# Moving one buffer by 128 bytes: split weights that begin 192 bytes past a multiple of 512 in place of 64

## The reference

```
# block 1, two layers: attention, then a pooling mixer, each followed by an MLP
x = x + moba_attention(rms_norm(x, g), w_qkv, w_o, cos, sin)
x = x + squared_relu_mlp(rms_norm(x, g), w_up, w_down)     # 1024 -> 4096 -> 1024
x = x + pool_mixer(rms_norm(x, g), w_groups, scale)
x = x + squared_relu_mlp(rms_norm(x, g), w_up, w_down)
x = rms_norm(x, g)
# block 2: a state-space branch and a latent-attention branch on one input projection,
# gated and merged; then cross attention to a memory of 256 rows;
# then 32 experts, each 1024 -> 256 -> 1024, two for each token; then a last norm
act = silu(t @ w_gate[e]) * (t @ w_up[e]) * combine
```

## Time and profile before

| | |
|---|---|
| three runs | 1241.28, 1235.68, 1241.53 us; median 1241.28 |
| the profiled execution | 1234.28 us, of which the span is 1232.5 |
| mean granted clock of TensorE | 0.993 |
| TensorE busy | 1179.9 us (96%), 9056 matmuls |
| VectorE busy | 783.6 us (64%) |
| ScalarE busy | 608.3 us (49%) |
| DMA | 270.28 MB, mean 219 GB/s |

### The profile page before, as it was taken

How to read it: one execution, slowest core, us unless ns; L and a number is a source line. 1 busy time by engine, 2 the same in 40 slices (tenths; PEclk the granted TensorE clock), 3 DMA queues, 4 the chain that set the end, 5 groups by cost and what they waited for, 6 DMA issues and landing times. The chain is left out here.

```text
span 1232.5 us, 22410 instructions
## 1 busy us (share of the span) xinstructions
PE 1179.9 (96%) x9056; PEld 1000.1 (81%) x9056; DVE 783.6 (64%) x1316; ACT 608.3 (49%) x993; POOL 100.0 (8%) x102
## 2 busy tenths in 40 slices
PE   9999999999999999999999989999999999999992
PEld 7989999999999999899999988899999833333320
DVE  6876655566755566999899889879655552221213
ACT  6665554455544554767655576665554331111101
POOL 0000100000200000000000030010100004341301
PEclk9999999999999999999999999999999999999997
DMA  9654566564456656445444384365543999999993
GB/s 303 203 172 137 189 189 198 185 196 146 162 181 195 193 182 197 137 152 173 155 137 138 109 274 139 104 205 168 186 160 124 421 360 412 417 413 414 412 404 130
DMA packets 161045, 270.28 MB, mean 219 GB/s; under 512 B 17625, under 2 KB 126142, under 8 KB 156862
## 3 DMA queue, kind: packets, MB, share of 16 engines
q1 hardware_dynamic: 149872, 260.53, 60.6%
q0 software_dynamic: 10720, 8.42, 2.3%
q10 hardware_dynamic: 366, 0.12, 0.0%
HBM read 287.89 MB, written 13.63 MB: 245 GB/s over the span
## 5 line engine op out<-in xcount | busy, mean ns | idle before, releaser
L2128 DVE TENSOR_TENSOR weights_parts<-ring,weights_parts 128x1024 fp32r<-128x1024 f32 (+3 forms) x312 | 363.5, 1185 | 138.4 <-ACT weights_parts L1546 138.0
L1546 ACT ACTIVATE weights_parts<-ring 128x1024 fp32r<-128x1024 f32 (+3 forms) x312 | 309.1, 1011 | 144.6 <-PE psum L885 143.9
L883 PE MATMUL psum<-xnorm_parts,weights_parts 128*128 128x256 f32 x852 | 243.4, 286 | 6.8 <-DVE arena L2531 3.2
L884 PE MATMUL psum<-xnorm_parts,weights_parts 128*128 128x256 f32 x852 | 237.5, 279 | 0.0
L885 PE MATMUL psum<-xnorm_parts,weights_parts 128*128 128x256 f32 x852 | 237.5, 279 | 0.0
L883 PE MATMUL psum<-expert_cols,weights_parts 128*128 128x256 f32 (+1 forms) x688 | 192.5, 280 | 3.5 <-DVE expert_cols L2146 2.2
L884 PE MATMUL psum<-expert_cols,weights_parts 128*128 128x256 f32 (+1 forms) x688 | 190.1, 276 | 0.0
L885 PE MATMUL psum<-expert_cols,weights_parts 128*128 128x256 f32 (+1 forms) x688 | 190.1, 276 | 0.0
L883 PE MATMUL psum<-hidden_parts,weights_parts 128*128 128x256 f32 x640 | 178.7, 279 | 3.0 <-DVE hidden_parts L2599 1.7
L884 PE MATMUL psum<-hidden_parts,weights_parts 128*128 128x256 f32 x640 | 177.1, 277 | 0.0
L885 PE MATMUL psum<-hidden_parts,weights_parts 128*128 128x256 f32 x640 | 177.1, 277 | 0.0
(11 more groups left out here) (452 smaller groups left out, 1723.8 us busy)
## 6 DMA issues: line engine op xcount, KB each, us to landing
ring<-in_mlp_w_up SPq DMA_DIRECT2D x32, 1024.0 KB, 5.4
ring<-in_mlp_w_down SPq DMA_DIRECT2D x32, 1024.0 KB, 4.8
ring<-in_w_in SPq DMA_DIRECT2D x30, 1024.0 KB, 5.1
ring<-in_attn_w_qkv SPq DMA_DIRECT2D x12, 1024.0 KB, 6.0
expert_raw<-in_w_exp_gate SPq DMA_DIRECT2D x22, 512.0 KB
expert_raw<-in_w_exp_up SPq DMA_DIRECT2D x22, 512.0 KB
ring<-in_w_exp_down SPq DMA_DIRECT2D x9, 1024.0 KB
expert_raw<-in_w_exp_down SPq DMA_DIRECT2D x9, 1024.0 KB
```

Of the source, the lines that this page charges most:

```text
L883: pe.matmul(out, lh, rh, start=start, stop=False, **more)
L884: pe.matmul(out, lh, rl, start=False, stop=False, **more)
L1546: ins = act.activation(high, src, ACT.Copy)
L2128: ins = dve.tensor_tensor(low, src, high.bitcast(F32), ALU.subtract)
```

## The change

The call that makes `dskip_all` moves ahead of the two that make the weights buffer. With its 128 bytes in front, `weights_parts` and `expert_weights` begin at byte 193,728 of a partition (378 x 512 + 192) and no longer at 193,600 (378 x 512 + 64). `dskip_all` itself goes from byte 226,368 to 193,600. `ssd_par` and all behind it, and all ahead of `dskip_all`, keep their addresses. No instruction changes its place on any engine: 6034 rows of TensorE, 950 of VectorE, 731 of ScalarE, 71 of GpSimd and 271 of SyncE stand in the order in which they stood.

```
--- before.py
+++ after.py
@@ -394,10 +394,10 @@
         results = sb("results", [P, M_END - M_COLS])
         arena_rest = sb("arena_rest", [P, ARENA - M_END])
         half_rows = sb("half_rows", [P, 2, 2 * MORE], I32)
+        dskip_all = sb("dskip_all", [P, SH])
         with nc.sbuf_tensor("expert_weights", [P, 2 * UNITS * UNIT], F32) as w_plain:
             pass
         w_parts = sb("weights_parts", [P, 2 * UNITS * UNIT], F32R)
-        dskip_all = sb("dskip_all", [P, SH])
         ssd_par = sb("ssd_par", [SH, 4])
         std_col = sb("std_col", [P, 2, TB])
         gain_both = sb("gain_both", [P, KT])
```

## The result

The changed kernel has a median of 1247.84 us over 8 runs (1240.26 to 1252.12), the kernel before 1237.97 over 8 (1232.67 to 1242.39). The ratio is 1.0084, with a 95% interval from 1.0059 to 1.0108. I had forecast no change, with 1239 us and a chance of 0.14 for slower.

A forecast was written before the change was run, and what follows sets the result against it. TensorE was taken to set the pace ahead of the expert stage, DMA queues from 1000 us. Terms for TensorE, VectorE with ScalarE, and DMA summed to 0, keeping 1234.28 us; 1239 was forecast, between two groups of runs, range 1230 to 1250.

The forecast's parts named there:

- What bounds the kernel: TensorE sets the pace ahead of the expert stage, DMA queues from 1000 us; TensorE's changes ahead pass on nearly in full.
- VectorE, ScalarE, the expert stage's matmuls at 0: Splitting the weights and streaming them in the expert stage cost 0; VectorE and ScalarE within 0.5 us each way.
- DMA at 0: Expert loads into the weights buffer take no longer: 0, with ends of -2.7 and +2.7 us.
- the sign: In the expert stage, 412 GB/s from 1000 to 1100 us would show the forecast right.
- My estimate of 1.6 us of 244: Expert-stage writes into the weights buffer 1.6 us slower if the page's rule for reads held; not taken into the sum.
- TensorE, split products, at 0: The 6996 split matmuls keep their two paces, 113.3 and 117.7 ns: 0, with ends of +21 and -9.5 us.
- 64 against 0 as a bound for 192: Rows comparing starts 64 and 0 on TensorE, VectorE and ScalarE, differing by 0 to -10 ns, stood in for start 192.
- The slower rival: Fast split matmuls turn slow, above all the MLP's: 13.5 us, 1252 us; all 4800 quick ones 21 us, 1260; chance 0.18.
- The slow share of 2170: Of 6996 split matmuls, some 2170 have the slow pace, 281 ns duration, and would stay near that count.
- The marks: Signs of right or wrong, such as MLP's 1008 matmuls in 114.24 us (right) or 118.6 us (wrong, the slower rival).

The follow-up runs named there:

- the first small kernel: Split matmuls alone, computation left out, each stretch behind a wait, stationary and moving starts each 0 to 448 bytes in steps of 64; 113.3 to 120.0 ns per matmul.
- the version with two starts: Kernel before with a 128-byte gap between high and low weights, high parts at 64, low at 192: 1233.60 us, ratio 0.9929; again 1232.06 us, 0.9964.
- the one at 0: Kernel before with half_rows laid behind the weights, so the weights begin at 0 like the other large buffers: 1265.01 us, ratio 1.0201.
- the one at 320: Kernel before with a gap of 256 bytes ahead of the weights, which begin at 320, others at 0: 1239.85 us, ratio 1.0022.

## Why the prediction was wrong

- **What bounds the kernel**: right. TensorE's pace ahead of the expert stage is what the change touched, and between 0.7 and 0.9 of it reached the end.
- **VectorE, ScalarE, the expert stage's matmuls at 0**: right, 1241, 1054 and 592 ns. **DMA at 0**: right for this buffer. The first 100 us of the sign, 1000 to 1100, have 404 GB/s in place of 412, 394 up to 1050 us and 414 behind it, as the stage begins later. What the stage takes is the same: from the first to the last matmul from the weights buffer 187.5 and 187.7 us in two executions before, 187.6 and 187.8 in two after. My estimate of 1.6 us of 244, from the Trainium skill's page DMA: Bandwidth & Descriptors, section "How a descriptor splits into AXI transactions", would be 1.2 us of this span, and the traces don't bear it out.
- **TensorE, split products, at 0**: this step failed. It said "One start that has both paces says that something else picks between them", and went from there to a price of 0 with a weight of 0.62. Something else does pick between two paces, the moment of entry. But the start decides which paces there are to pick from, and how often each is picked: at class 64 both, at class 192 nearly always 117.8 from a wait or a short lead (0 of 96), at 0 and 128 the quick one never (0 of 191 stretches in the first small kernel). Two outcomes at one setting only show that the setting doesn't fix the outcome; they leave open that it sets the odds.
- **64 against 0 as a bound for 192**: the nearest rows were the wrong ones. All of them (592 ns, 1217 ns, 620 ns) are of work in which TensorE doesn't read two SBUF operands in this close order, or which isn't TensorE's at all. In the split products no row of before had stationary and moving operand at another distance than 64 or -64, and I did not say that this left 0 and 128, now known to be 5 to 7 ns worse than the quick pace, without any row. What I also missed: with the period of 256, -64 is 192, the distance to which the change takes the stationary weights. The products with the weights moving were rows of it. By their start times 398 of 469 ran slow before, against 1685 of 6402 with the weights stationary; the earlier trace rows show it as means of 278 and 279 ns. They are short stretches, and even at 64, after the change, 270 and 353 of them ran slow, so this alone would not have settled the price.
- **The slower rival** was the right mechanism: "the places that are fast now can turn slow, above all the MLP". Its price, 13.5 us for the MLP and 21 for everything, is that of the second execution of the changed kernel, where the matmuls took 19.7 us more (117.53 against 114.71 ns, x 6996) and the time was 17.9 us longer. In the first, the MLP's loops stayed quick and it was 8.9 and 6.0. The median lies between. I had given it 0.18 because no row said what picks a pace; that lack should have counted for it as much as against it.
- **The slow share of 2170**, worked out from means of durations, was 2091 by the start times. The same sum wouldn't do after: at 192 the slow pace has 279 ns, not 281.
- **The marks**: "1008 matmuls of the MLP in 118.6 us" didn't come in the first trace and did in the second; with one trace of the changed kernel, that mark would have spoken for the wrong case.
- **The time**: 1247.84 lies inside the range of 1230 to 1250, but the direction was missed.

## What to carry to other kernels

Where a kernel reloads the stationary operand for every matmul, look at the starts of the stationary and the moving operand modulo 256 bytes, and sweep them with a kernel of a few hundred bare matmuls: here the first such run ranked the starts 0, 128, 192 and 64 as the full kernel did, over a range of 2%, and a later one found the version with two starts, 0.4 to 0.7% under the kernel before. Count matmul starts in equal stretches, since means of durations hide two paces. And when one setting shows two outcomes, ask what sets their odds before giving the setting a price of nothing.

## What the runs showed that I had not expected

- The pace of back-to-back 128x128 by 256 split matmuls depended on (stationary start - moving start) mod 256: 120.0 ns at 0, 113.3 or 117.8 at 64, 118.2 to 119.1 at 128, 117.8 and sometimes 113.3 at 192. At 64 it was not the difference alone that picked.
- Of 16 starts in steps of 16 bytes, 113.3 ns came only at 64 and 192.
- Which of two paces a stretch takes is settled within its first few matmuls and then kept, for over 1000 of them in the MLP; it differs between executions of one program. I take this for the main part of the scatter of 10 us in the runs before (the version with two starts spreads over 4 us, the one at 0, which has one pace, over 2.5 us in six runs, and the one at 320, which has two, over 17 us in twelve), which the line through the executions supports and no run proves.
- With all large buffers at 128 in place of 0 the expert stage, which the DMA sets, took 4.4 and 4.7 us more (404 and 407 in place of 414 GB/s); with the weights buffer moved alone it took no more.
- What inside TensorE or SBUF makes the classes stays open; no run here shows it.
